# Twenty of 24 modulation slabs computed inside the panels and the feed-forward instead of before them

## The reference, cut to what matters

```python
def trunk_layer(x, cvec, l, P, hg_lower, cache):
    mod = jax.nn.silu(cvec) @ P['w_mod'][l] + P['b_mod'][l]      # (1024) @ (1024, 6*1024)
    mod = mod.reshape(cvec.shape[0], 1, N_MOD, D_MODEL)
    g = P['norm_g'][l]
    h = rmsnorm(x, g[0]) * (1.0 + mod[:, :, 1]) + mod[:, :, 0]
    m, ctx = token_mixers(h, l, P, hg_lower, cache)              # u = h @ w_in[l], three mixers, w_br, gates, w_o
    x = x + mod[:, :, 2] * rmsnorm(m, g[1])
    h = rmsnorm(x, g[2]) * (1.0 + mod[:, :, 4]) + mod[:, :, 3]
    if l % 2 == 0:
        f = swiglu(h, P['w_ffn_gu'][l // 2], P['w_ffn_down'][l // 2])
    else:
        f = moe(h, ...)                                          # top 2 of 8 experts
    x = x + mod[:, :, 5] * rmsnorm(f, g[3])
    return x, ctx
```

## Time and profile before

| | us |
|---|---|
| median of 3 runs (2015.32 to 2020.06) | 2017.97 |
| profiled execution: first to last instruction | 2017.5 |
| front: until the first matmul of panel 0 | 179.9 |
| panels 0 to 7 of layer 0, roughly | 180 to 280 |
| dense feed-forward | 522 to 718 |
| panels of layer 1 start | 746 |

### The profile page before, as it was taken

One profiled execution on the slowest core, in us unless ns is written; L12 is line 12 of the kernel. 1 busy time (PEld: TensorE's weight loads), 2 busy tenths in 40 slices (PEclk: granted clock), 3 DMA queues, 4 the chain that ended last, 5 costly groups with the idle time before them and its releaser, 6 DMA issues.

```text
span 2017.5 us, 21065 instructions
## 1 busy us (share of the span) xinstructions
PE 1838.1 (91%) x8174; PEld 1421.4 (70%) x8175; DVE 1257.1 (62%) x1077; ACT 988.4 (49%) x929; POOL 126.1 (6%) x78
## 2 busy tenths in 40 slices
PE   8999999988699959999976898989898989898996
PEld 1225888876588848888865687878787878787773
DVE  1103558873444445579843686868686868696872
ACT  2102445333444354353332676767676767675751
POOL 1000203310000001013200000000000000000000
PEclk9999999998899969999977899999999999999998
DMA  9886454424244334544323597979797979797950
GB/s 401 293 305 250 167 198 167 156 105 158 114 188 188 125 115 167 198 167 159 134 94 146 195 348 307 368 277 375 278 374 272 374 278 375 275 378 267 359 209 21
DMA packets 55794, 470.21 MB, mean 233 GB/s; under 512 B 6352, under 2 KB 6400, under 8 KB 8496
## 3 DMA queue, kind: packets, MB, share of 16 engines
q1 hardware_dynamic: 52848, 458.25, 59.5%
q0 software_dynamic: 2880, 11.02, 1.3%
HBM read 465.05 MB, written 4.19 MB: 233 GB/s over the span
## 4 chain that ended last, share of the span: by engine, by line
PE 88%; DVE 4%; ACT 4%; issue 3%; DMA 0%; POOL 0%; POOLq 0%; ACTq 0%; DVEq 0%
PE ps L918 24%; PE ps L920 23%; PE ps L919 23%; PE ps L893 8%; ACT w_hi L705 2%; PE ps L1088 2%; PE ps L980 1%; PE ps L1310 1%; PE ps L1050 1%; DVE ring_lo L1603 1%; PE ps L912 1%; PE ps L960 1%; ACT ring_lo L694 0%; DMA ring<-in_w_mod 0%; ACT wide L621 0%
## 5 line engine op out<-in xcount | busy, mean ns | idle before, releaser
L1603 DVE TENSOR_TENSOR ring_lo<-ring,w_hi 128x2048 fp32r<-128x2048 f32 x297 | 679.9, 2292 | 232.1 <-ACT w_hi L705 232.1
L918 PE MATMUL ps<-ring_lo,h_hi 128*128 128x512 f32 x1520 | 610.5, 402 | 31.1 <-issue 25.1
L705 ACT ACTIVATE w_hi<-ring 128x2048 fp32r<-128x2048 f32 x297 | 568.0, 1913 | 107.0 <-PE ps L920 97.6
L918 PEld LDWEIGHTS ps<-ring_lo,h_hi 128*128 128x128 f32 x1520 | 289.4, 190 | 93.7 <-issue 34.0
L1542 DVE TENSOR_TENSOR ring_lo<-ring,ring_lo 128x2048 fp32r<-128x2048 f32 x76 | 182.6, 2405 | 267.0 <-ACT ring_lo L694 266.4
L920 PE MATMUL ps<-w_hi,h_hi 128*128 128x512 f32 x880 | 346.2, 393 | 0.0
L919 PE MATMUL ps<-w_hi,h_lo 128*128 128x512 f32 x880 | 345.7, 393 | 0.0
L694 ACT ACTIVATE ring_lo<-ring 128x2048 fp32r<-128x2048 f32 x92 | 176.1, 1916 | 325.8 <-PE ps L920 213.3
L920 PE MATMUL ps<-ring_lo,h_hi 128*128 128x512 f32 x640 | 251.8, 393 | 0.0
L919 PE MATMUL ps<-ring_lo,h_lo 128*128 128x512 f32 x640 | 251.7, 393 | 0.0
L918 PE MATMUL ps<-ring_lo,act_hi 128*128 128x512 f32 x440 | 181.9, 413 | 41.6 <-DVE ring_lo L1603 41.6
(11 more groups left out here) (263 smaller groups left out, 1489.9 us busy)
## 6 DMA issues: line engine op xcount, KB each, us to landing
ring<-in_w_ff SPq DMA_DIRECT2D x297, 1024.0 KB, 6.9
ring<-in_w_in SPq DMA_DIRECT2D x36, 2048.0 KB, 8.0
ring<-in_w_mod SPq DMA_DIRECT2D x24, 2048.0 KB, 8.1
ring<-in_w_br SPq DMA_DIRECT2D x6, 2048.0 KB, 7.8
ring<-in_w_o SPq DMA_DIRECT2D x4, 2048.0 KB, 8.0
out<-state_out POOLq DMA_DIRECT2D x4, 512.0 KB, 4.9
x_sb<-in_x POOLq DMA_DIRECT2D x1, 1024.0 KB, 26.8
state<-in_s_ret POOLq DMA_DIRECT2D x2, 512.0 KB, 22.3
```

What stands on the lines that cost most here:

```text
L705: A(w_hi[p], ring[i % SLOTS][:, p * UNIT:(p + 1) * UNIT], ACT.Copy).then_inc(hi_ready[p], 1)
L918: mm(out, a_hi, b_lo, start=start, stop=False, skip_group_check=True)
L1603: V.tensor_tensor(ring_lo[i % SLOTS][:, part], ring[i % SLOTS][:, part], w_hi[p].bitcast(F32), ALU.subtract)\
```

## The change

Only the four slabs of layer 0 that panel 0 needs stay in the front (`modulate_first`). Layer 0's other eight are computed in panels 0 to 7 of layer 0, one a panel, between its two halves (`modulate_mix`). Layer 1's first four are computed in steps 2, 4, 6 and 8 of the dense feed-forward, between the two parts of the gate-and-up product (`modulate_ffn`), and its other eight in panels 0 to 7 of layer 1. Every one of them now writes 32 rows, one column group of the array (`QUAD`), in place of 12 or 36.

Since the slabs are apart in time, each has its own accumulation in a PSUM bank that the pieces leave free at that moment, with waits for it, and DVE adds it to rows in SBUF (`add_mod`). The rows are turned in four batches (front; panel 8 of layer 0; step 9 of the feed-forward; panel 8 of layer 1), by an ordinary float32 matmul with the identity in place of a transpose. ACT's copy goes.

The slabs no longer pass through the ring, except the first four. In the panels a slab is loaded as two halves into an area under `w_hi1` and one in `u2` (`mod_units`: SP asks for it behind the next panel slab, once the modulation slab before it is used), in the feed-forward into two areas in `u` (`mod_slab`). The loop in SP's front goes. The ring's order keeps its parity for layer 1 by three skipped slots; `wo` slabs sit one slot apart. Setup semaphores of ACT and DVE are merged into two counters with the same order of work. The scaling coefficients of gates, and of the second sub-layer, are waited for in both layers.

```diff
 NSLAB_MOD = 12
 MOD_FIRST = 4
-MOD_TURNS = L * NSLAB_MOD // SLOTS
-MOD_SPLIT = -(-MOD_FIRST // SLOTS) * SLOTS
-MOD_GROUPS = [range(0, MOD_SPLIT), range(MOD_SPLIT, L * NSLAB_MOD)]
-COND_PAD = 2 * max(len(r) for r in MOD_GROUPS) - 2
+MOD_LATER = NSLAB_MOD - MOD_FIRST
+QUAD = 32
+COND_PAD = 2 * MOD_LATER - 2
+
+MOD_BATCHES = [(0, 0, MOD_FIRST), (0, MOD_FIRST, NSLAB_MOD), (1, 0, MOD_FIRST), (1, MOD_FIRST, NSLAB_MOD)]
+MIX_MOD_BANK = [4, 4, 4, 4, 6, 6, 4, 6]
+FFN_MOD_STEP = [2, 4, 6, 8]
+FFN_MOD_TURN = 9
...
 def layer_slabs(l):
     slabs = []
     if l == 0:
-        slabs = [("mod", n // NSLAB_MOD, n % NSLAB_MOD) for n in range(L * NSLAB_MOD)]
+        slabs = [("mod", 0, n) for n in range(MOD_FIRST)]
     for j in range(NWIN):
         slabs.append(("win", l, j))
         if j in BR_AFTER:
             slabs.append(("br", l, BR_AFTER[j]))
-    return slabs + [("wo", l, 0), ("skip", l, 0), ("wo", l, 1)] + [("skip", l, 1)] * (l == L - 1)
+    if l == 0:
+        return slabs + [("wo", l, 0), ("wo", l, 1)] + [("skip", l, i) for i in range(3)]
+    return slabs + [("wo", l, 0), ("skip", l, 0), ("wo", l, 1), ("skip", l, 1)]
...
+        (mod_w0,), (w_hi1,) = shared([("mod_w0", UNIT)], [("w_hi1", UNIT)])
...
+        mod_w = [mod_w0, u2[:, 2 * D:4 * D]]
+        mod_wide = [u[:, 3 * D:7 * D], u[:, 7 * D:11 * D]]
...
+        cond_pad = sb("cond_pad", KD * (COND_PAD + QUAD)).rearrange("p (k c) -> p k c", k=KD)
+        mod_rows = sb("mod_rows", 512)
...
+        def mod_count(l, n):
+
+            return NSLAB_MOD * l + n + 1
+
+        def mod_rows_count(l, n):
+
+            if l == 0:
+                return 1 if n < MOD_FIRST else n - MOD_FIRST + 2
+            return MOD_LATER + 2 + n
...
+            def mod_units(l, n):
+
+                if n > MOD_FIRST or l:
+                    sp.wait_ge(mod_done, mod_count(l, n) - 1)
+                if n == MOD_FIRST and l:
+                    sp.wait_ge(gu_done, NFS)
+                for b in range(2):
+                    src = w_mod[l * NSLAB_MOD + n][:, b * UNIT:(b + 1) * UNIT]
+                    sp.dma_start(mod_w[b], src).then_inc(mod_in, 16)
+
+            def mod_slab(n):
+
+                if n >= 2:
+                    sp.wait_ge(mod_done, mod_count(1, n - 2))
+                sp.dma_start(mod_wide[n % 2], w_mod[NSLAB_MOD + n]).then_inc(mod_wide_in[n % 2], 16)
+
...
             for l in range(L):
-                slabs = layer_slabs(l)
-                if l == 0:
...
-                    with sp.Fori(1, MOD_TURNS) as t:
-                        for s in range(SLOTS):
-                            sp.wait_ge(mod_done, t * SLOTS + (s - SLOTS + 1))
-                            sp.dma_start(ring[s][:, 0:KD * 512], w_mod[t * SLOTS + s]).then_inc(slab_in[s], 16)
-                    slabs = slabs[MOD_TURNS * SLOTS:]
-                for key in slabs:
+                for key in layer_slabs(l):
                     if key[0] != "skip":
                         load(key)
+                    if key[0] == "win" and 1 <= key[2] <= MOD_LATER:
+                        mod_units(l, MOD_FIRST + key[2] - 1)
                 if l == 0:
                     for i in range(NFS):
                         load(("ffn", 0, i))
+                        if i + 1 in FFN_MOD_STEP:
+                            mod_slab(FFN_MOD_STEP.index(i + 1))
...
-            def copy_mod(part):
-
-                slabs = MOD_GROUPS[part]
-                act.wait_ge(mod_done, slabs[-1] + 1)
-                A(mod_rows[0:2 * len(slabs), part, :], ps[0:2 * len(slabs), part, :], ACT.Copy).then_inc(mod_copied, 1)
...
-            def modulate(part):
-
-
-                slabs = MOD_GROUPS[part]
-                height = 2 * len(slabs)
-                for i, n in enumerate(slabs):
-                    s, u, _ = plan[("mod", n // NSLAB_MOD, n % NSLAB_MOD)]
+            def mod_blocks(n, w, blocks, bank, start, stop):
+
+                at = COND_PAD - 2 * n
+                for k in blocks:
+                    ins = mm(ps[0:QUAD, bank, :], cond_pad[:, k, at:at + QUAD], w[:, k - blocks[0], :],
+                             start=start and k == 0, stop=stop and k == KD - 1, skip_group_check=True)
+                return ins
+
+            def modulate_first():
+
+
+                for n in range(MOD_FIRST):
+                    s, u, _ = plan[("mod", 0, n)]
                     pe.wait_ge(slab_in[s], 16 * (u + 1))
                     w = ring[s][:, 0:KD * 512].rearrange("p (k c) -> p k c", k=KD)
-                    at = COND_PAD - 2 * i
-                    for k in range(KD):
-                        ins = mm(ps[0:height, part, :], cond_pad[:, k, at:at + height], w[:, k, :],
-                                 start=(i == 0 and k == 0), stop=(n == slabs[-1] and k == KD - 1), skip_group_check=True)
-                    ins.then_inc(mod_done, 1)
-
-            def turn_mod(part):
-
-                height = 2 * len(MOD_GROUPS[part])
-                pe.wait_ge(mod_copied, part + 1)
+                    mod_blocks(n, w, range(KD), 0, n == 0, n == MOD_FIRST - 1).then_inc(mod_done, 1)
+
+            def modulate_mix(l, j):
+
+                if j:
+                    pe.wait_ge(mod_added, mod_rows_count(l, MOD_FIRST + j - 1))
+                if j == 4:
+                    pe.wait_ge(t_read_dve, 5 * l + 2)
+                if j == 6:
+                    pe.wait_ge(ro_read, l + 1)
+                if j == 7:
+                    pe.wait_ge(t_read_dve, 5 * l + 4)
+                pe.wait_ge(mod_in, 32 * (MOD_LATER * l + j + 1))
+                for b in range(2):
+                    w = mod_w[b].rearrange("p (k c) -> p k c", k=4)
+                    ins = mod_blocks(j, w, range(4 * b, 4 * b + 4), MIX_MOD_BANK[j], b == 0, b == 1)
+                ins.then_inc(mod_done, 1)
+
+            def modulate_ffn(n, i):
+
+                pe.wait_ge(actT_ready, i)
+                pe.wait_ge(mod_wide_in[n % 2], 16 * (n // 2 + 1))
+                w = mod_wide[n % 2].rearrange("p (k c) -> p k c", k=KD)
+                mod_blocks(n, w, range(KD), 6, True, True).then_inc(mod_done, 1)
+
+            def turn_mod(batch, bank):
+
+                l, first, end = MOD_BATCHES[batch]
+                width = 2 * (end - first)
+                pe.wait_ge(mod_added, mod_rows_count(l, end - 1))
                 for c in range(4):
-                    ins = nc.tensor.transpose(ps[:, 2 + part, c * height:(c + 1) * height],
-                                              mod_rows[0:height, part, c * P:(c + 1) * P], ident[0:height, 0:height])
+                    ins = mm(ps[:, bank, c * width:(c + 1) * width], mod_rows[0:QUAD, c * P:(c + 1) * P], ident[0:QUAD, 0:width],
+                             start=True, stop=True)
                 ins.then_inc(mod_turned, 1)
...
-                    pe.wait_ge(mod_read, 1)
                 for half in range(2):
+                    if half and j < MOD_LATER:
+                        modulate_mix(l, j)
+                    if half and j == MOD_LATER:
+                        turn_mod(2 * l + 1, 6)
                     hi, lo = unit(l, STEP["win", j], half, 4)
...
                 pe.wait_ge(win_read, NWIN * l + STAGED[q] + 1)
                 if q < 2:
                     pe.wait_ge(rope_ready, 2 * l + q + 1)
+                if q == 2:
+                    pe.wait_ge(mod_added, mod_rows_count(l, MOD_FIRST + 5))
+                if q == 4:
+                    pe.wait_ge(mod_read, 2 * l + 2)
                 if 1 <= q <= 5:
...
-                if l == 0 and n == 0:
-                    pe.wait_ge(mod_rest, 1)
+                if n == 0:
+                    pe.wait_ge(mod_rest, l + 1)
...
+                        if mods and i - 1 in FFN_MOD_STEP:
+                            pe.wait_ge(mod_added, mod_rows_count(1, FFN_MOD_STEP.index(i - 1)))
+                        if mods and i - 1 == FFN_MOD_TURN:
+                            pe.wait_ge(mod_read, 3)
...
+                            if mods and p and i in FFN_MOD_STEP:
+                                modulate_ffn(FFN_MOD_STEP.index(i), i)
+                            if mods and p and i == FFN_MOD_TURN:
+                                pe.wait_ge(actT_ready, i)
+                                turn_mod(2, 6)
                             pe.wait_ge(lo_ready[p], base + (i + 1))
                             pe.wait_ge(hi_ready[p], base + (i + 1))
...
+                    pe.wait_ge(mod_added, mod_rows_count(l, MOD_FIRST + 3))
...
+                    pe.wait_ge(mod_added, mod_rows_count(l, MOD_FIRST + 6))
...
-            pe.wait_ge(cond_ready, 1)
-            modulate(0)
+            pe.wait_ge(setup_act, 1)
+            modulate_first()
             turn_rows(0, 0)
-            turn_mod(0)
-            modulate(1)
-            turn_mod(1)
+            turn_mod(0, 2)
...
+            def add_mod(l, n, bank):
+
+                dve.wait_ge(mod_done, mod_count(l, n))
+                at = mod_rows_count(l, n)
```

(69 more changed lines are left out.)

55 lines of the change are left out of this document (23 added, 32 removed).

## The result

| | before | after |
|---|---|---|
| median of 4 runs, us | 2017.42 | 2041.98 |
| lowest to highest, us | 2015.32 to 2020.06 | 2039.51 to 2043.68 |
| span of the profiled execution, us | 2017.5 | 2037.7 |
| start of panel 0, us | 179.93 | 56.65 |

A forecast was written before the change was run, and what follows sets the result against it. TensorE was taken as the bound, busy 91% of the span. Front +19.9, turns +1.8 and insertions +2.0 sum to +23.7 us on a span of 2017.5; with 0.5 between span and median, 2041.5 us, range 2030 to 2056.

The forecast's parts named there:

- the front: Before panel 0: 137.5 us of slabs leave, but PE waits and panel 0 starts cold at 59.6 us; net +19.9 us.
- the turns: Modulation rows turned between products on PE: one turn becomes three, 0.6 us each, +1.8 us.
- the insertions: Twenty times PE leaves the products for a slab's 16 small instructions: 0.1 us each, +2.0 us.
- The price of a slab: Modulation matmuls in front and receiving stretches: 16 instructions of 0.4296 us, 6.87 us of PE a slab; twenty moved net 0.
- The rival of starved panels: Panels: a mod slab beside the win slab lands later than 11.8 us; 4 us late in 14 panels, +56, 2097; chance 0.07.
- the one of overlap: Receiving stretches: slabs run partly beside products, costing below 5.7 us each, so faster; all hidden 1904 us; chance 0.06.
- the high end: Front: x lands late, and one slab ahead of the bias adds up to 6 us; +26 us for the front.
- The cold start: Start of panel 0: a dozen matmuls at about 0.44 us in place of 0.23 after PE idles; 2.7 us.
- Clock: Rival after insertions: small matmuls let the clock fall, a cold dozen of products each, 2.4 us; +48, 2090; chance 0.03.
- Waits 0: Panels and feed-forward: waits for slab loads, DVE's add and actT_ready hold nothing up; 3.7 us of slack for loads; 0.
- the rest 0: Merged setup semaphores, smaller memset, fewer skipped slots and layer 1's shortened modulation sit beside work that ends earlier; 0.
- Little loss: Rival in the panels: PE's records hide 24 us of waits that slabs fill, 1.2 us a slab; 2018 us; chance 0.04.

The follow-up runs named there:

- the quarter slab: Kernel after the change, but each of the 20 later slabs issues only 4 of its 16 matmul instructions; 1944.86 us, ratio 0.9633 to the kernel before.
- the run above: Kernel after the change, with the fourth modulation slab asked for only when x has landed; 2040.87 us, ratio 1.0114 to the kernel before.
- the two kernels built from the one before: Kernel before, with the last 3 or 6 slabs of layer 1 moved from the front into PE's idle stretches; 1996.61 us with 3, 1972.37 us with 6.
- the run with 128 columns: Kernel after the change, each modulation matmul 128 columns wide (the array's full width) in place of 32; 2038.4 us, ratio 1.0102 to the kernel before.

## Why the prediction was right

The sum held, on a right mechanism, but with three terms that were off and cancelled: the front by -4.4 us, the turns by +1.8, the insertions by +4.4. That the total came within 2 us is in part luck.

- *The price of a slab, 0.4296 us an instruction in both places*: right. The groups have 592 to 595 ns, the chain 6.98 with an edge. A panel with a slab recurs 7.19 us later than before, though, and not 6.9 to 7.0: the edges below. No wait for `mod_w` or `u`: in the panels the loads landed 5.0 and 7.1 us after their issue, where 11.8 or more were at hand. The rival of starved panels has fallen with that, and the one of overlap with the quarter slab.
- *The front, +19.9*: right in mechanism, 4.4 too dear. PE idles from 39.9 to 42.2 and from 46.8 to 56.65, for the waits named; the price measured is 56.65 - 179.93 + 137.5 = +14.2, and 1.3 of cold products. The step that failed first is the one before the transposes: it took the end of DVE's scaling from the old timeline (45.2). That timeline hangs on the constants: the first instruction of DVE's setup waits for the last of them, `level_mask`, which landed 20.6 us after its issue before and 17.5 after. The timelines of DVE, before and after:
```profile
25.84 0.17 DVE L1335 TENSOR_TENSOR lbw<-lbr 128x8 f32<-128x8 f32 x1 [24.39 <-DMA level_mask<-in_levels]
...
22.75 0.17 DVE L1391 TENSOR_TENSOR lbw<-lbr 128x8 f32<-128x8 f32 x1 [21.50 <-DMA level_mask<-in_levels]
```
  Everything behind it came 3.0 us earlier (squares at 29.54 in place of 32.59, scaling over at 42.16). x, which the prediction made the high end, landed 3.0 us earlier too (23.8 against 26.8), each time just as ACT's setup ended. It alone would not have brought this: with x 4 us earlier still, in the run above, the squares came no earlier. In all nine other profiles `level_mask` took 17.4 to 18.1 us, also in the two kernels built from the one before. So these 3.0 us may be chance of the one execution profiled before, and are not shown to come from the change.
  The cold start was six products and 1.3 us, not a dozen and 2.7. The chain between, 14.4 from the scaling's end (45.2 to 59.6) by forecast, took 14.5.
- *Turns, 3 x 0.6*: 0.99 for the eight instructions in the chain, and 0.2 at the product behind, about 1.2 each: 3.6 in place of 1.8. I had counted four matmuls; each is two instructions.
- *Insertions, 20 x 0.1*: 0.32 each, outside the bound of 0.25, so 6.4 us in place of 2.0. I had taken the edge from the turn of 8 between panels, whose tile is as wide as the products', which the run with 128 columns showed to be the wrong row: there the edge is nil. For this, the rule in TensorEngine Tiling (Array Packing) of the Trainium skill, section Tiling Modes, Key Properties, that a change of the tiling mode drains TensorE, was the better guide. The trace agrees in size: 0.29 to 0.32 us per trip there and back, or 6 us over twenty, against the 7 of the prediction's estimate. That a drain is what the time goes to is not shown.
- *Clock*: of the products behind an insertion only the first takes 0.43, and that is the edge; no cold stretch follows. The stretch of the panels stays at 1.00, which is 2.4 GHz:
```profile
62.00:260.00 198.00, 198.00 (x830) 131.34 (x829) 85.79 (x93) 63.18 (x67) 17.73 (x14) 1.00 0.54 199
```
- *Waits 0, DVE's longer modulation 0, the rest 0*: right within 0.6 us a stage, by the ledger, where the clock is the same.
- *Little loss* asked for hidden waits in the panels; the panels are longer by the slab and its edges, so there are none.

Measured by the ledger: 14.2 + 1.3 + 6.4 + 3.6 = 25.5 us in the steps of the change, 23.7 forecast, less 5.3 in the stages without slabs, which is the clock in the profiled pair. The medians, over which such scatter averages, differ by 24.6, with 20 to 27 by the ratio. The largest error was hence one that no term had: a single pair of executions is good to some 5 us here. It touched the base too. The prediction put 0.5 us between span and time, from one span and the median of other executions; where both are known for one execution it is 1.7 to 3.3. The span of 2017.5 it started from was some 2 us longer than a typical one, and the two slips cancel.

## What to carry to other kernels

Moving matmuls out of a block that keeps TensorE full pays only if they land in an idle stretch of TensorE; into another full stretch they carry their whole time, and what they covered is laid open. Before moving, follow the chain that the block covers, and ask of each place whether PE is idle there: here a slab in a gap was worth 7.5 us between the medians (22.4 / 3 and 45.7 / 6), more than its own 6.87, since it also keeps the clock at 2.4 GHz for what follows (transposes in 1.97 us in place of 3.68). Take the price of an edge from a row with the same tile sizes on either side.

## What the runs showed of the hardware that was not expected

- Twelve, 32, 36 and 128 columns of float32 weights cost the same 0.4296 us a matmul of 512 columns moved, but a block of 32-column matmuls between products of 128 pays about 0.3 us a visit, and one of 128 columns nothing. At the way out the weight load of the first product differs. Timelines of the weight loads, kernel after and full width:
```profile
107.71 0.19 PEld L958 LDWEIGHTS ps<-ring_lo,h_hi 128*128 128x128 f32 x1 [0.84 <-issue]
...
108.37 0.19 PEld L959 LDWEIGHTS ps<-ring_lo,h_hi 128*128 128x128 f32 x1 [0.24 <-issue]
```
  By the chain the slab ends at 107.78 in the first and at 108.96 in the second. So behind 32 columns the load starts 0.07 us before the slab is over, and behind 128 columns 0.59 us before. The 0.1 us on the way in has no such row.
- The length of a cold start varies at equal work: in one and the same place six products in one execution of the kernel after (411.27 us) and eleven in the other (413.92), and sixteen transposes 3.46 and 2.85 us. Stages made of short bursts scatter by up to 2.5 us, and with them the span of the whole kernel, by 5 us (2037.7 and 2042.8).
- How soon x lands went with when the fourth slab was asked for: 26.8 us after its own issue with the slab asked for at 17.98 us, 23.7 with 19.13, and 19.8 with the slab held back until x was there. That last run held everything else fixed (24.8 in the kernel after on the same chip). Whether the earlier landing in the kernel after comes from that alone wasn't tried, and holding the slab back did not move `level_mask` (17.8 and 17.9).
